# RWKV scan in an encoder layer: level products merged in pairs, state decay moved to another engine

## The reference

```python
def step(state, inp):
    r_t, w_t, k_t, v_t, kk_t, a_t = inp
    sa = jnp.einsum('bhvk,bhk->bhv', state, -kk_t)
    state = (state * w_t[:, :, None, :] + sa[..., None] * (kk_t * a_t)[:, :, None, :]
             + v_t[..., None] * k_t[:, :, None, :])
    return state, jnp.einsum('bhvk,bhk->bhv', state, r_t)
```

## Time and profile before

| | |
|---|---|
| median of 3 runs | 2628.55 us (2627.21 to 2631.51) |
| the profiled execution | 2627.98 us, its span 2626.2 us |
| busy in the span | PE 2399.8 (91%), PEld 1864.5 (71%), DVE 1562.1 (59%), ACT 1080.5 (41%), POOL 775.4 (30%) |
| `wkv_scan` within it | about 830 to 1312 us |
| its ten full passes, j = 0 to 9 | 894.15 to 1252.57 us, 358.42 us |

### The profile page before, as it was taken

The page is one execution under the profiler, slowest core; times in us unless marked ns, Lnnn a source line. Parts: engine busy times, 40 slices in busy tenths (PEclk is TensorE's granted clock), DMA queues, the critical chain, the costliest instruction groups (busy, mean ns, idle before and its releaser), DMA issues. The chain is left out here.

```text
span 2626.2 us, 53374 instructions
## 1 busy us (share of the span) xinstructions
PE 2399.8 (91%) x22291; PEld 1864.5 (71%) x22291; DVE 1562.1 (59%) x2402; ACT 1080.5 (41%) x1951; POOL 775.4 (30%) x511
## 2 busy tenths in 40 slices
PE   5799999999997899999989799998998996999997
PEld 2488887788886888888878666666876884555554
DVE  3544458976663445555377566666885886544433
ACT  4311123343442566656465455553122221544443
POOL 1122244545451455444213200001300000444443
PEclk8999999999998999999999999999998997999998
DMA  8522224344435123332044611104755446899994
GB/s 343 210 81 80 80 89 156 119 149 153 157 119 186 55 74 86 95 100 73 22 153 118 161 33 34 29 12 162 237 158 212 151 148 234 318 359 347 353 322 113
DMA packets 196291, 399.28 MB, mean 152 GB/s; under 512 B 38698, under 2 KB 104010, under 8 KB 182994
## 3 DMA queue, kind: packets, MB, share of 16 engines
q1 hardware_dynamic: 173876, 322.58, 36.2%
q0 software_dynamic: 12960, 41.82, 6.0%
q10 hardware_dynamic: 9216, 31.46, 3.0%
HBM read 294.57 MB, written 106.48 MB: 153 GB/s over the span
## 5 line engine op out<-in xcount | busy, mean ns | idle before, releaser
L99 PE MATMUL ps_in<-h_t_low,w_in_high 128*128 128x512 f32 x960 | 378.7, 394 | 2.1 <-PEq L79 2.1
L100 PE MATMUL ps_in<-h_t_high,w_in_low 128*128 128x512 f32 x960 | 373.9, 389 | 0.0
L101 PE MATMUL ps_in<-h_t_high,w_in_high 128*128 128x512 f32 x960 | 373.8, 389 | 0.0
L99 PEld LDWEIGHTS ps_in<-h_t_low,w_in_high 128*128 128x128 f32 x960 | 180.2, 188 | 44.5 <-issue 5.6
L1275 POOL TENSOR_TENSOR wkv_levels<-wkv_nt,level_mask 128x1024 f32<-128x1024 f32 x60 | 140.5, 2359 | 230.0 <-ACT wkv_nt L1220 230.0
L101 PEld LDWEIGHTS ps_in<-h_t_high,w_in_high 128*128 128x128 f32 x960 | 180.2, 188 | 38.0
L100 PEld LDWEIGHTS ps_in<-h_t_high,w_in_low 128*128 128x128 f32 x960 | 180.3, 188 | 35.7
L607 ACT COPY p_row<-ps_in 128x512 f32<-128x512 f32 x72 | 42.4, 588 | 293.4 <-PE ps_in L101 256.3
L3078 PE MATMUL ps_xy<-w_tile,hidden_turned 128*128 128x512 f32 x272 | 123.6, 597 | 16.4 <-DMA w_tile<-in_w 15.0
L498 POOL CAST w_in_high<-w_in_tile 128x1024 fp32r<-128x1024 f32 x39 | 45.7, 1171 | 299.3 <-PE ps_in L101 297.2
L705 DVE TENSOR_SCALAR p_mixed<-p_row,mu_centre 128x1537 f32<-128x1537 f32 x24 | 35.3, 1473 | 148.0 <-ACT p_row L607 147.8
(11 more groups left out here) (432 smaller groups left out, 6221.0 us busy)
## 6 DMA issues: line engine op xcount, KB each, us to landing
merged_t<-in_w SPq DMA_DIRECT2D x36, 1024.0 KB, 11.2
w_tile<-in_w SPq DMA_DIRECT2D x34, 1024.0 KB, 15.4
w_now<-in_w SPq DMA_DIRECT2D x30, 1024.0 KB, 15.8
w_ada_tile<-in_w_ada SPq DMA_DIRECT2D x12, 2048.0 KB, 9.2
wkv_in<-wkv_out SPq DMA_DIRECT2D x24, 1024.0 KB, 3.9
w_in_tile<-in_w_in SPq DMA_DIRECT2D x40, 512.0 KB, 3.6
p_t<-p_mixed ACTq DMA_DIRECT2D x24, 512.0 KB, 2.7
gates<-p_mixed ACTq DMA_DIRECT2D x16, 768.0 KB, 4.6
```

The lines of the kernel that those rows point to most:

```text
L99: nc.tensor.matmul(out, w[0], x[1], start=start, stop=False)
L100: nc.tensor.matmul(out, w[1], x[0], start=False, stop=False)
L101: return nc.tensor.matmul(out, w[0], x[0], start=False, stop=stop)
```

## The change

Four edits in `wkv_scan`.

1. Level products. `x` and a new `xt_wide` get a second slot for each chunk, so that the moving operand is block-diagonal over the two chunks: chunk `c`'s 64 partitions are filled only in slot `c`, the rest is zero (set once at the start by four memsets on DVE, with PE waiting for them before its first such product). One product of 128 rows by 64 columns with 64 moving columns then does what two of 64 by 64 with 32 did. `level_z` and `level_xz` have 16 products each (32 matmuls in the profile) in place of 32 (64).
2. To fill these operands, DVE's transpose becomes two instructions of 64 partitions, and ACT's `copy_over` (two copies) becomes `widen` (four copies of the same size).
3. The second decay goes from ACT to POOL: two instructions of 128 by 256 in place of eight of 128 by 64, both placed at the head of POOL's pass. `next_state` becomes two multiplications of 128 by 256 out of PSUM, a wait for them (`s0_part`), and one addition of 128 by 512.
4. `bk` has two buffers in place of three, and its load for tile `j+3` stands behind the first store and the load of `ar` in SP's pass, where it waits for `turn_bk` of tile `j+1`.

```diff
-        AR, BK, LB = 3, 3, 3
+        AR, BK, LB = 3, 2, 3
-        x = s.sb("wkv_x", [P, 2, 2 * H, BLK])
+        x = s.sb("wkv_x", [P, 2, 2, 2 * H, BLK])
-        xt_over = s.sb("wkv_xt_over", [P, H, BLK])
+        xt_wide = s.sb("wkv_xt_wide", [P, 2, 2, H, BLK])
-        level_tiles = [(d, f, c, b) for d in range(2) for f in range(RF) for c, b in ((0, 0), (1, 1), (0, 1), (1, 0))]
+        column_halves = [(d, f, a) for d in range(2) for f in range(RF) for a in range(2)]
...
             for j in range(N):
                 if j + 2 < N:
                     load_v(j + 2)
-                if j + 3 < N:
-                    load_bk(j + 3)
...
                 store(j, 0)
                 if j + 3 < N:
                     load_ar(j + 3)
+                    load_bk(j + 3)
                 store(j, 1)
...
-                for d, f, c, b in level_tiles:
+                for d, f, b in column_halves:
                     h = H * d + RF * b + f
-                    mm = nc.tensor.matmul(LV[half(b), c, 0, RF * d + f], lev[half(c), l, h], x[half(c), i % 2, h], start=True, stop=True)
+                    mm = nc.tensor.matmul(LV[half(b), 0, :, RF * d + f], lev[:, l, h], x[:, i % 2, :, h], start=True, stop=True)
...
-                for d, f, c, b in level_tiles:
-                    right = xt[half(c), i % 2, H * d + RF * b + f] if b == c else xt_over[half(b), RF * d + f]
-                    mm = nc.tensor.matmul(LV[half(c), b, 1, RF * d + f], z[half(b), c, RF * d + f], right, start=True, stop=True)
+                for d, f, c in column_halves:
+                    mm = nc.tensor.matmul(LV[half(c), 1, :, RF * d + f], z[:, c, RF * d + f], xt_wide[:, c, :, RF * d + f], start=True, stop=True)
...
-            def copy_over(i, l):
+            def widen(i, l):
...
                 for b in range(2):
-                    ins = nc.scalar.copy(xt_over[half(b)].rearrange("p (d f) t -> p d (f t)", d=2), by_side(xt[half(1 - b), i % 2])[:, :, b])
-                ins.then_inc(m["xt_over"], 1)
+                    for c in range(2):
+                        ins = nc.scalar.copy(xt_wide[half(b), c, b].rearrange("p (d f) t -> p d (f t)", d=2), by_side(xt[half(c), i % 2])[:, :, b])
+                ins.then_inc(m["xt_wide"], 1)
...
+            def decay_again(i, k):
+                if k == 1 and i + 1 in RUN_ENDS:
+                    return
+                pool.wait_ge(m["s0_ready"], 2 * i + k + 1)
+                for d in range(2):
+                    c = chunk(k, d)
+                    ins = nc.gpsimd.tensor_tensor(s1[:, 1 - c], s0[:, c], decay(i, k, d).to_broadcast([P, RF, CH]), ALU.mult)
+                ins.then_inc(m["s1_ready"], 1)
...
             for j in range(-2, N):
+                if j >= 0:
+                    decay_again(j, 0)
+                    decay_again(j, 1)
...
             def turned(dst, src):
                 flat = lambda a: a.rearrange("p h t -> p (h t)")
-                return nc.vector.transpose(flat(dst), flat(src))
+                for c in range(2):
+                    ins = nc.vector.transpose(flat(dst[half(c), c]), flat(src[half(c)]))
+                return ins
...
-                        for f in range(RF):
-                            ins = nc.vector.scalar_tensor_tensor(out=s0[:, 1 - c, f], in0=S[:, c, CH * f:CH * f + CH], scalar=decay(i, k, d, f),
-                                                                 in1=s1[:, 1 - c, f], op0=ALU.mult, op1=ALU.add)
-                    ins.then_inc(m["s0_ready"], 1)
+                        ins = nc.vector.tensor_tensor(s0[:, 1 - c], S[:, c].rearrange("p (f t) -> p f t", f=RF), decay(i, k, d).to_broadcast([P, RF, CH]), ALU.mult)
+                    ins.then_inc(m["s0_part"], 1)
+                    dve.wait_ge(m["s0_part"], 2 * i + k + 1 - int(i >= RUNS[1][0]))
+                    nc.vector.tensor_tensor(s0[:], s0[:], s1[:], ALU.add).then_inc(m["s0_ready"], 1)
...
+            for c in range(2):
+                nc.vector.memset(x[half(c), :, 1 - c], 0.0).then_inc(m["zeros"], 1)
+                nc.vector.memset(xt_wide[half(c), :, 1 - c], 0.0).then_inc(m["zeros"], 1)
```

More of the change, by code:

```diff
@@ L915, in _ @@
                 load_ar(i)
-                load_bk(i)
+                if i < BK:
+                    load_bk(i)
                 if i < 1:
@@ L995, in level_z @@
                 pe.wait_ge(m["x_ready"], LEVELS * i + l)
[L996 removed]
+                if i == 0 and l == 1:
+                    pe.wait_ge(m["zeros"], 4)
+                for d, f, b in column_halves:
                     h = H * d + RF * b + f
[L998 removed]
+                    mm = nc.tensor.matmul(LV[half(b), 0, :, RF * d + f], lev[:, l, h], x[:, i % 2, :, h], start=True, stop=True)
                 mm.then_inc(m["z_full"], 1)
@@ L1016, in half_product @@
                             a, b = quad(c, d), quad(c, 1 - d)
-                            mm = nc.tensor.matmul(LV[b, d, 1, h], nt[a, i % 2, H * d + h, BLK * (1 - d):BLK * (1 - d) + BLK], x[a, i % 2, H * d + h],
+                            mm = nc.tensor.matmul(LV[b, 1, d, h], nt[a, i % 2, H * d + h, BLK * (1 - d):BLK * (1 - d) + BLK], x[a, i % 2, c, H * d + h],
                                                   start=True, stop=True)
@@ L1202, in keep_u @@
                 ins.then_inc(m["u_kept"], 1)
-            def decay_again(i, k):
-                if k == 1 and i + 1 in RUN_ENDS:
-                    return
-                act.wait_ge(m["s0_ready"], 2 * i + k + 1)
-                for d in range(2):
-                    c = chunk(k, d)
-                    for f in range(RF):
-                        ins = nc.scalar.mul(s1[:, 1 - c, f], s0[:, c, f], decay(i, k, d, f))
-                ins.then_inc(m["s1_ready"], 1)
             def keep_nt(i):
@@ L1231, in keep_half @@
                 act.wait_ge(m["half_full"], i + 1)
-                nc.scalar.copy(half_inv[:].rearrange("p (d h) t -> p d h t", d=2), LV[:, :, 1]).then_inc(m["half_kept"], 1)
+                nc.scalar.copy(half_inv[:].rearrange("p (d h) t -> p d h t", d=2), LV[:, 1]).then_inc(m["half_kept"], 1)
             for j in range(-2, N):
@@ L1236, in _ @@
                 if inner:
-                    copy_over(j + 1, 1)
+                    widen(j + 1, 1)
                     keep_z(j + 1, 1)
                 if seq:
-                    decay_again(j, 0)
                     keep_u(j, 0)
                 if inner:
-                    copy_over(j + 1, 2)
+                    widen(j + 1, 2)
                     keep_v(j + 1)
                     keep_z(j + 1, 2)
-                if seq:
-                    decay_again(j, 1)
                 if inner:
-                    copy_over(j + 1, 3)
+                    widen(j + 1, 3)
                     keep_z(j + 1, 3)
@@ L1255, in _ @@
                 if inner:
-                    copy_over(j + 1, 4)
+                    widen(j + 1, 4)
                     keep_bk(j + 1, 0)
```

20 lines of the change are left out of this document (10 added, 10 removed).

## The result

The changed kernel is slower. Timed against the kernel before it took 2661.16 us (median of 4, 2649.67 to 2663.35) beside 2629.82: ratio 1.0111, interval [1.0081, 1.0142]. Timed a second time, in five rounds, it took 2647.81 us (2643.27 to 2656.81) beside 2631.61: 1.0070 [1.0049, 1.0090]. So 0.7 to 1.1% slower. The profiled execution took 2649.67 us, its span is 2647.8.

The account below looks back on a forecast made before the run. PE's queue sets the time, with ten passes losing 25.4 us to late instructions and the slow clock after them. 2628.0 + 25.4 (longer passes) - 17 (stream relief) + 4 (clock) = 2640.4, forecast 2641 us, range 2624 to 2660.

Parts of the forecast that it names:

- Part 1, nothing on the array: Level products on PE: a wide group takes 0.96 to 0.98 us without a shape change, saving nothing on the array.
- The rival of wide products at half the time: Level products: 96 products each less by half of 0.96 us, at most half kept, about 2610 us; chance 0.02.
- Parts 1 and 2, +2.24 us a pass: Undisturbed pass of the scan: 0.82 + 0.10 + 0.50 + 0.82 us added, 35.5 in place of 33.3.
- The terms on copies and transposes: Operand filling on ACT and DVE: copies add 0.82 us in each of two chains, the level 2 transpose 0.50.
- The two passes at the ends: Pass -1 and pass 10 of the scan: +1.5 us each.
- Part 3, nothing: Decays on POOL and next_state on DVE: both stay in slack, costing nothing; the addition takes 0.69 or 1.06 us.
- Part 4, "Nothing on the path": Later bk load and the memsets: 18 us available for a load of 5, DVE idle for the memsets, no cost.
- What comes back from the instruction stream, -17 and +4: PE: a quarter fewer instructions recovers 17 us of 25.4; the slow clock behind longer waits before products(0,0) costs 4.
- The clock rival: PE's longer wait lowers the clock in most passes: ten times 1.7 us more, less the 4, 2655 or above; chance 0.15.
- No relief: PE's stops have another cause than the number of instructions and stay: 2654 us; chance 0.13.
- Balance: Instruction stream's relief is full (-27 us) and the chains cost as worked out: 2627 to 2632, no change; chance 0.18.
- faster: Relief in full and the added 2.24 us a pass partly absorbed: 2616 us at 1.2 a pass; chance 0.12.

Follow-up runs that it names:

- half_copies: Changed kernel with only the two copies across the partitions, both transposes kept (inverse not the reference's): ratio 0.9966 to the kernel before.
- one_turn: Changed kernel with one transpose of 128 partitions in place of two of 64, all four copies kept (values not the reference's): ratio 1.0069 to the kernel before.
- lean_wide: Changed kernel with only the two cross-partition copies and one transpose of 128 partitions (values not the reference's): ratio 0.9947 to the kernel before.
- state_only: Kernel before with only the decay on POOL and the new state in three operations: ratio 1.0001 to the kernel before.
- products_only: Changed kernel with the second decay back on ACT and the new state in DVE's eight joint operations: ratio 1.0072 to the kernel before.
- loads_only: Kernel before with only two bk buffers and the bk load for tile j+3 behind the load of ar: ratio 1.0109 to the kernel before.
- bk_head: Changed kernel with the bk load moved to the head of SP's pass, for tile j+2, two buffers kept: ratio 1.0056 to the kernel before.
- whole_again: Changed kernel unaltered, timed a second time: 2647.81 us, ratio 1.0070 to the kernel before.
- filler: Changed kernel with eight dummy matmuls on PE ahead of products(0,0), filling the wait for keep_v: ratio 1.0058 to the kernel before.
- v_first: Changed kernel with keep_v ahead of widen(2) on ACT: 2636.41 us, ratio 0.9999 to the kernel before.
- bk_head_v_first: Changed kernel with the bk load for tile j+2 at the head of SP's pass and keep_v ahead of widen(2): 2636.18 us, ratio 0.9991 to the kernel before.

## Why the prediction was right or wrong

It said 2641 us, slower by 0.5%; the medians are 2648 and 2661. The sign was right and the parts of an undisturbed pass nearly so, the size was 7 to 20 us too low. The first median lies 1 us above the upper end of the range, but the kernel before took 1.3 us longer beside it than in the rows of the prediction: 1.0111, where the upper end is 1.0120.

- **Part 1, nothing on the array.** Right: 0.95 us to a group of the same shape and 1.08 to another. The rival of wide products at half the time is refuted. It was the one from the Trainium skill, page "TensorEngine Tiling (Array Packing)", section "Instruction Overhead"; the trace disagrees with what I drew from that page, 0.95 us where half of 0.96 was to be.
- **Parts 1 and 2, +2.24 us a pass.** Right in kind, 0.36 short: an undisturbed pass is 35.9 in place of 33.3, +2.6. The terms on copies and transposes came true: both chains of copies together 1.6 (half_copies; forecast 1.64), the transposes 0.5 (one_turn; forecast 0.50), both together 2.3 (lean_wide; forecast 2.14). What is left without them is 0.3, where the only other term was 0.10 for shape changes; no run takes these 0.3 apart. (The 689 and 683 ns that the prediction calls copies are DVE's arithmetic on 64 and 128 partitions out of PSUM; that a transpose of 64 takes as long as one of 128 is shown now by its own row, 705 ns.) The two passes at the ends cost 0.6 and 0.5 us in place of 1.5 each, and the pass after them 1.3 less.
- **Part 3, nothing.** Right in its effect (state_only, products_only). POOL's decay is 0.62 us where I took 0.74. The addition was mis-sized: 1.33 us on average and 2.25 at most, above the 1.06 that I had as its upper bound, since it waits out a mask of POOL's. Only slack hid it.
- **Part 4, "Nothing on the path".** As a rule for this load that was wrong, and in this kernel it held by a cover that the working doesn't have. I had seen that the load would run beside `half_product` and `cross_product`, "whose 128 small matmuls use up instructions fastest", and gave it no price. loads_only priced it at 1.09% on the old kernel. In the new one 0.1% or so is left of it (bk_head), most likely since it asks for fewer instructions. That the term fits here is luck.
- **What comes back from the instruction stream, -17 and +4.** This is the step that went wrong: the relief was put far too high and the clock too low. Ten passes lost 25.4 us to disturbance before, and now 380.2 - 359 = 21.2 (whole_again: 18.8). I had 12.4. The relief itself exists: packets fell by a quarter, stops from 18.4 to 8.9 us. But it is half of the stops and not two thirds of all disturbance, and I had counted the clock's recovery with it, while the slow clock rose by 13.6 us, worth 6.8, where I had put +4 in all. 9.5 less in stops and 6.8 more by the clock make a gain of 2.7, where I had 13; measured is 4.2 (whole_again: 10.1 and 5.1 make 5.0; measured 6.6).
- **The clock rival** (2655 or above, chance 0.15) was right in kind. It held for half the waits (26 of 50) and not for most; filler, v_first and the 90 passes without the long wait show that the wait for `keep_v` is the cause. That the first median lies in its range is in part luck: half of the slow clock in the profiled execution stands behind stops and not behind the wait. The forecast and this rival are one story with two sizes, and the measured time lies between them and at its end.
- **No relief**: refuted as a mechanism by the packets, since stops end with them and both became fewer; as a size, net relief of 4 us in ten passes is nearer to it than to the forecast's 13. The Trainium skill, page "Runtime: NRT & Kernel Launch", section "Instruction fetch mechanics", has the crossing of a 16 KB boundary as "mostly hidden". By count the traces agree, as PE ran on at 67 of 83 borders before and at 52 of 63 after; in time the rest is not small, 18.4 and 8.9 us of stops in about 360 and 380 us.
- **Balance and faster**: both needed full relief and got a sixth to a quarter of it. lean_wide and half_copies show when they would have come true: with the copies at half their number the kernel is 0.3% faster than before.

The working against its profiled execution: forecast 2640.4, measured 2649.7. Undisturbed passes +3.6, disturbance +8.8, the passes at the ends -2.0, the pass after them -1.3: +9.1 of the 9.3.

What stays open: why about half of the equal waits brought the slow clock and the others did not, where the 0.3 us of a pass beside copies and transposes come from, and why the first timing was 13 us above the second.

## What to carry to other kernels

Filling a block-diagonal operand costs copies, and what they cost is decided by the queue position and not by the engine's load: ACT was less busy than before and PE waited twice as long, until `keep_v` was moved ahead of the copies. Before an edit on an engine with slack, look at which of its instructions PE waits for next, and put that one first. A wait of nearly 2 us on PE was to be priced twice here, for itself and for the half clock behind it; and a transfer that no engine waits for cost a per cent of the old kernel, when it ran beside the groups that use up instructions fastest.

## What the runs showed of the hardware

- A product of 128 rows by 64 columns with 64 moving columns took as long as two of 64 by 64 with 32: 32 matmuls start to start in 0.95 us, and 64 of half the rows in four places of the array in 0.96. Merging block products saved instructions and no array time.
- Both kinds of pause led to the lower clock of 1.2 GHz: waits of 1.9 us (3.4 us of it behind 26 of 50 in five kernels; behind waits of 1.1 us or less in none of 90) and some stops inside a group, 0.97 to 1.7 us from start to start in the changed kernel and bk_head_v_first (3.4 to 10.2 us).
- PE stopped in the middle of groups whose operands were ready, at borders of the 16 KB packets of its instructions, and went on 1.19 to 1.59 us after a packet had landed (158 of 160 stops). Moving one load beside small matmuls took the stops from 18.4 to 29.4 us and the time at half clock from 20.5 to 105.8.
- An addition of two SBUF operands, 128 by 512, took 0.69 us on DVE alone; started inside one of POOL's masks it ended 0.54 to 0.58 us after the mask in 69 of 69 cases, up to 2.55 us in all; started 0.2 us ahead of one it took 0.69 in 21 of 21; and POOL's next operation (L1281) took 1.61 in place of 1.27. The Trainium skill, page "GPSIMD Engine Reference", section "1. Specifications", says that the two share an SBUF interface and collide when DVE's instruction has two SBUF inputs. The trace agrees.
- DVE's transpose takes 705 ns for 64 partitions and about 0.7 us for 128; splitting one by partitions doubles its cost.
